# Gate and up of a feed-forward by Strassen's scheme, with its activations stored to memory between two stages

## What is computed

```python
def conv_ffn(h, conv_prev, w_gate_l, w_up_l, w_conv_l, b_conv_l, w_down_l):
    t_ = h.shape[1]
    g = jnp.einsum('btd,df->btf', h, w_gate_l)
    u = jnp.einsum('btd,df->btf', h, w_up_l)
    gp = jnp.concatenate([conv_prev.astype(g.dtype), g], axis=1)
    gc = sum(gp[:, j:j + t_] * w_conv_l[j] for j in range(CONV_W)) + b_conv_l
    a = (jax.nn.gelu(gc.astype(jnp.float32)) * u.astype(jnp.float32)).astype(h.dtype)
    return jnp.einsum('btf,fd->btd', a, w_down_l), gp[:, -(CONV_W - 1):]
```

## Time and profile before

| | us |
|---|---|
| median of 3 runs (3435.79 to 3442.96) | 3439.86 |
| the profiled execution | 3438.7 |
| its span in the profile | 3437.1 |
| PE busy in the span | 3172.0 (92%), 19515 matmuls |
| DVE busy | 2157.2 (63%) |
| ACT busy | 1555.2 (45%) |
| POOL busy | 703.7 (20%) |
| DMA | 614.89 MB, mean 179 GB/s |
| mean granted clock | 0.966 |

### The profile page before, as it was taken

One profiled execution on the slowest core, in us unless ns is written; L12 is line 12 of the kernel. 1 busy time (PEld: TensorE's weight loads), 2 busy tenths in 40 slices (PEclk: granted clock), 3 DMA queues, 4 the chain that ended last, 5 costly groups with the idle time before them and its releaser, 6 DMA issues. The chain is left out here.

```text
span 3437.1 us, 58878 instructions
## 1 busy us (share of the span) xinstructions
PE 3172.0 (92%) x19515; PEld 2946.1 (86%) x19515; DVE 2157.2 (63%) x4569; ACT 1555.2 (45%) x3302; POOL 703.7 (20%) x532
## 2 busy tenths in 40 slices
PE   6989989799989997876997999999999999999997
PEld 5989989698989994443785999999999999999997
DVE  7787776578777773333995664566366446636754
ACT  5555544588867773322543333333333343333332
POOL 4464554254510003333452000000000000000000
PEclk8999999899999998998998999999999999999999
DMA  4546556727366769997586674576467557655442
GB/s 139 155 156 184 163 156 180 201 46 157 72 147 156 180 173 293 311 318 249 163 245 190 181 231 144 162 246 211 134 206 232 162 154 234 204 159 145 122 115 81
DMA packets 670664, 614.89 MB, mean 179 GB/s; under 512 B 39849, under 2 KB 580866, under 8 KB 665282
## 3 DMA queue, kind: packets, MB, share of 16 engines
q1 hardware_dynamic: 640726, 479.02, 49.6%
q10 hardware_dynamic: 10606, 69.86, 6.0%
q0 software_dynamic: 19104, 63.06, 5.7%
HBM read 512.41 MB, written 166.40 MB: 197 GB/s over the span
## 5 line engine op out<-in xcount | busy, mean ns | idle before, releaser
L2743 DVE TENSOR_TENSOR ff_wl<-ff_wr,ff_wh 128x1024 fp32r<-128x1024 f32 (+2 forms) x380 | 403.9, 1079 | 248.3 <-ACT ff_wh L2675 248.1
L2675 ACT ACTIVATE ff_wh<-ff_wr 128x1024 fp32r<-128x1024 f32 (+2 forms) x380 | 348.8, 938 | 207.1 <-PE ff_d L2600 126.3
L2598 PE MATMUL ff_g<-ld_mem,ff_wh 128*128 128x416 f32 x880 | 311.0, 353 | 20.0 <-DVE ff_wl L2743 19.8
L2598 PE MATMUL ff_u<-ld_mem,ff_wh 128*128 128x416 f32 x880 | 310.1, 352 | 2.7 <-DVE ff_wl L2743 2.7
L2598 PE MATMUL ff_d<-ff_ah,ff_wh 128*128 128x416 f32 x880 | 312.2, 355 | 0.0
L2600 PE MATMUL ff_d<-ff_ah,ff_wl 128*128 128x416 f32 x880 | 310.0, 352 | 0.0
L2600 PE MATMUL ff_g<-ld_mem,ff_wl 128*128 128x416 f32 x880 | 309.9, 352 | 0.0
L2600 PE MATMUL ff_u<-ld_mem,ff_wl 128*128 128x416 f32 x880 | 308.8, 351 | 0.0
L2599 PE MATMUL ff_g<-ld_mem,ff_wh 128*128 128x416 f32 x880 | 308.6, 351 | 0.0
L2599 PE MATMUL ff_u<-ld_mem,ff_wh 128*128 128x416 f32 x880 | 307.7, 350 | 0.0
L2599 PE MATMUL ff_d<-ff_al,ff_wh 128*128 128x416 f32 x880 | 307.5, 349 | 0.0
(11 more groups left out here) (312 smaller groups left out, 8171.2 us busy)
## 6 DMA issues: line engine op xcount, KB each, us to landing
...
bx_kca<-in_cache_a_k SPq DMA_DIRECT2D x128, 256.0 KB, 13.5
sa_vca<-in_cache_a_v POOLq DMA_DIRECT2D x128, 256.0 KB, 8.0
...
```

Source lines behind the costliest of these rows:

```text
L2598: pe.matmul(dst[:, 0:FG], wh[:, k, c], src[0][:, c0 + c], start=first and c == 0, stop=False)
L2675: act.activation(wh[:, slot, 0:size], wr[:, slot, 0:size], ACT.Copy).then_inc(w_hi, 1)
L2743: dve.tensor_tensor(wl[:, slot, 0:size], wr[:, slot, 0:size], wh[:, slot, 0:size].bitcast(F32), ALU.subtract).then_inc(w_lo, 1)
```

## The change

The function `ffn` and its stage are taken out. In their place stand `ffn_up` (stage `fu`) and `ffn_down` (stage `fd`) inside an outer stage `fk`, which keeps what both need.

- `ffn_up` makes gate and up in the manner of the projection: three rounds of 704, 704 and 672 tokens, 22 quads in each (11 pairs of feature tiles, gate in the even quads and up in the odd ones), 84 matmuls in each quad. Unlike in the projection the sums of weights are made by DVE (`sums`, names `fu_sm`). So are the sums of tokens: of the four of the first round POOL makes three and DVE one; those of the second and third are made by DVE in quads 11, 13, 15 and 17 of the round before. The first tap is one ACT instruction with scale and bias (`first_tap`), gelu stays on ACT, taps 1 and 2 and the product of gate and up are DVE's, now 704 wide. The split of the product is gone from here. The finished activations go to a tensor `a` in memory (23.4 MB) by stores of SP (`send`). The code is unrolled. SP also issues the copies of the window caches (`roll_old`), one per quad, and later two per down tile in four of the five groups.
- `ffn_down` makes the down product as before: 5 groups of 416 tokens, 8 tiles, 22 chunks, 3 matmuls. Its input comes back from `a` in four parts per group (`load_a`), is split by ACT (`values_high`) and DVE into a ring of 5 parts (`RING`), and the parts of the weights are 6, 5, 6 and 5 chunks.
- The mix writes `h2T` as one float32 part: one copy by ACT and one by DVE for each token tile, one store. `hid` holds the first 704 tokens, unsplit; `ffn_up` makes the high and low parts of each of the seven token operands of a round itself.

```diff
-IN_PLACE = FG // P
+AHEAD = ROUNDS[0][1]
+IN_PLACE = AHEAD // P
...
+        self.hid = self.own("ahead_hid", [P, DC, AHEAD], 0)
...
-                    sp.wait_ge(low2, raised(2 * m + 2))
-                    for part, src in enumerate(staged):
-                        sp.dma_start(t["h2T"][part][:, :, m * P:m * P + r],
-                                     src[:, m % 2, :, 0:r]).then_inc(h_out[m % 2], 16)
+                    sp.wait_ge(kept_a, raised(m + 1))
+                    sp.wait_ge(kept_b, raised(m + 1))
+                    sp.dma_start(t["h2T"][:, :, m * P:m * P + r], staged[:, m % 2, :, 0:r]).then_inc(h_out[m % 2], 16)
                 if m == IN_PLACE:
-                    for part, src in enumerate(staged):
-                        sp.dma_start(hid[:, part, :, m * P:FG].bitcast(F32), src[:, m % 2, :, 0:FG - m * P]).then_inc(hid_in, 16)
+                    sp.dma_start(hid[:, :, m * P:AHEAD], staged[:, m % 2, :, 0:AHEAD - m * P]).then_inc(hid_in, 16)
...
+                act.wait_ge(turned2, raised(2 * m + 1))
+                act.activation(hidden_rows(m, 0), t2[0][:].rearrange("p (c x) -> p c x", c=4)[:, :, 0:r], ACT.Copy).then_inc(kept_a, 1)
...
+                dve.wait_ge(turned2, raised(2 * m + 2))
+                dve.tensor_copy(hidden_rows(m, 1), t2[1][:].rearrange("p (c x) -> p c x", c=4)[:, :, 0:r]).then_inc(kept_b, 1)
...
+ROLLS = [(kind, n, half) for n in range(DEC_B) for kind in range(2) for half in range(8)]
...
+def ffn_up(nc, t, ahead, keep):
...
+        ready = []
+        for i, (q, k) in enumerate(order):
+            ready.append(max([at[q - 1, k] if q >= 1 else -1, i - 7] + ready[-1:]))
+        T_ORDER = [(2, 1, 5, 3, 6, 7, 4)] + [(5, 2, 1, 3, 6, 7, 4)] * (NR - 1)
+        T_SUMS = (5, 7, 6, 4)
+        t_at = {(r, k): 7 * r + i for r in range(NR) for i, k in enumerate(T_ORDER[r])}
+        sum_at = {(r, k): 4 * r + i for r in range(NR) for i, k in enumerate(T_SUMS)}
+        S_ORDER = (5, 6, 3, 7)
...
+            def load_w(q, u):
+                if q >= TOTAL:
+                    return
+                n = 2 + u
+                if q >= n:
+                    sp.wait_ge(summed, raised(4 * (q - n) + 4))
+                    for k in ((4,) if u else (1, 2)):
+                        sp.wait_ge(w_lo, raised(at[q - n, k] + 1))
+                f = f_of(q, u) * P
+                sp.dma_start((rb if u else ra)[:, q % n], views[q % 2][:, :, f:f + P]).then_inc(w_in[u][q % n], 16)
+
+            def load_tokens(r):
+                at_, w = ROUNDS[r]
+                sp.wait_ge(t_lo, raised(7 * r))
+                for i in range(H_PARTS):
+                    c = slice(2 * i, 2 * i + 2)
+                    sp.dma_start(hraw[:, c, 0:w], t["h2T"][:, c, at_:at_ + w]).then_inc(h_in, 16)
+
+            def send(q):
+
+                for u in range(2):
+                    at_, w = ROUNDS[q // FNQ]
+                    sp.wait_ge(a_ok, raised(unit(q, u) + 1))
+                    sp.dma_start(t["a"][:, f_of(q, u), at_:at_ + w], ab[:, u, 0:w]).then_inc(keep.a_out[u], 16)
+
+            for u in range(2):
+                load_w(0, u)
+            for u in range(2):
+                load_w(1, u)
...
+            for q in range(TOTAL):
+                load_w(q + 2, 0)
+                if q % FNQ == 3 and q // FNQ + 1 < NR:
+                    load_tokens(q // FNQ + 1)
+                if q % 2 == 0 and q >= 4:
+                    send(q - 4)
+                roll_old(sp, t, keep, q)
+                load_w(q + 3, 1)
...
+            pool.memset(keep.carry[:], 0.0).then_inc(clear, 1)
+            token_sum(pool, 0, 7)
+            token_sum(pool, 0, 6)
+            token_sum(pool, 0, 4)
...
+            def tokens_high(r, k):
+                n = HALF[r]
+                if k in T_SUMS:
+                    act.wait_ge(t_sum, raised(sum_at[r, k] + 1))
+                elif r == 0:
+                    act.wait_ge(ahead.hid_in, 16)
+                else:
+                    act.wait_ge(h_in, raised(16 * H_PARTS * r))
+                if r > 0:
+                    act.wait_ge(mm, raised(at[FNQ * r - 1, k] + 1))
+                act.activation(oh[:, k - 1, :, 0:n], tokens_of(r, k), ACT.Copy).then_inc(t_hi, 1)
...
+            def first_tap(q, u):
+
+                f, w, first = f_of(q, u), prompt(q), aux_after(q, u) - (5 if last_round(q) else 2)
+                wait_unit(act, q, u)
...
+                    act.wait_ge(a_ok, raised(unit(q - 2, u) + 1))
+                n = span(q)
+                act.activation(ca[:, u, 0:n], gb[:, u, 0:n], ACT.Identity, scale=cw[:, 0, f:f + 1],
+                               bias=cw[:, TAPS, f:f + 1]).then_inc(tapped, 1)
+
+            def gelu(q, u):
+                n = span(q)
...
+            def beside(q, k):
+
+                if q % 2 == 1:
+                    if k == 5:
+                        first_tap(q - 1, 0)
+                    if k == 1:
+                        gelu(q - 1, 0)
+                if q % 2 == 0 and k == 4:
+                    first_tap(q, 1)
+                if q % 2 == 0 and q >= 2 and k == 2:
+                    gelu(q - 2, 1)
+
...
+            for j, k in enumerate(T_ORDER[0][0:5]):
+                tokens_high(0, k)
+                weights_high(j)
+            wait_mixed(act, ahead)
+            for i, (q, k) in enumerate(order):
+                read_product(q, k)
+                if i in EARLY:
+                    tokens_high(0, EARLY[i])
+                if next_round(i) is not None:
+                    tokens_high(next_round(i), k)
+                for x in range(len(order)):
+                    if ready[x] == i:
+                        weights_high(x)
+                beside(q, k)
...
+            def sums(q, k):
...
+            def beside(q, k):
+
+                if k == 3:
+                    sums(q + 2, 5)
+                for x, s_ in ((5, 6), (2, 3), (1, 7)):
+                    if k == (x if q else 5):
+                        sums(q + 1, s_)
+                if q % 2 == 1:
+                    for x, u, j in ((5, 0, 1), (2, 0, 2), (6, 1, 1)):
+                        if k == x:
+                            tap(q - 1, u, j)
+                elif q >= 2:
+                    if k == 5:
+                        tap(q - 2, 1, 2)
+                    if k == 2:
+                        gate(q - 2, 0)
+                    if k == 6:
+                        gate(q - 2, 1)
+                r, m = divmod(q, FNQ)
+                if r + 1 < NR and k == 1:
+                    for x, s_ in ((11, 5), (13, 7), (15, 6), (17, 4)):
+                        if m == x:
+                            token_sum(dve, r + 1, s_)
+
...
+D_PARTS = [6, 5, 6, 5]
+SLOTS = len(D_PARTS)
+RING = 5
...
+        PIECES = [(0, 0, 2), (0, 2, 6)] + [(p, 0, D_PARTS[p % SLOTS]) for p in range(1, PARTS)]
...
+            def load_a(p):
+                if p >= PARTS:
+                    return
+                g, j = divmod(p, SLOTS)
+                if j == 0:
+                    rounds = sum(at_ < (g + 1) * FG for at_, _ in ROUNDS)
+                    for u in range(2):
+                        sp.wait_ge(keep.a_out[u], 16 * PAIRS * rounds)
+                if p >= 2:
+                    sp.wait_ge(a_lo, raised(pieces_to[p - 2]))
+                c0 = FIRST[j]
+                sp.dma_start(ar[:, p % 2, 0:D_PARTS[j]], t["a"][:, c0:c0 + D_PARTS[j], g * FG:(g + 1) * FG]).then_inc(ar_in[p % 2], 16)
...
+                if g + 1 < NF:
+                    if d == 2:
+                        load_a(SLOTS * (g + 1))
+                        load_a(SLOTS * (g + 1) + 1)
+                    if d == 6:
+                        load_a(SLOTS * (g + 1) + 2)
+                    for i in range(2):
+                        roll_old(sp, t, keep, NR * FNQ + 2 * T + i)
...
+                weights_high(SLOTS * T + 2)
+                if d == 7:
+                    values_high(SLOTS * (g + 1) + 1)
+                if d == 0:
+                    if g == 0:
+                        values_high(2)
+                    values_high(SLOTS * g + 3)
+                if d == 3:
+                    values_high(SLOTS * (g + 1))
+                weights_high(SLOTS * T + 3)
+                if d == 7:
+                    values_high(SLOTS * (g + 1) + 2)
+                weights_high(SLOTS * T + 4)
+                weights_high(SLOTS * T + 5)
+                act.wait_ge(mm, raised(SLOTS * T + SLOTS))
...
-        ffn(nc, t, ahead)
+        with Stage(nc, "fk") as last:
+            keep = Kept(last)
+            ffn_up(nc, t, ahead, keep)
+            ffn_down(nc, t, ahead, keep)
```

960 lines of the change are left out of this document (574 added, 386 removed).

## The result

The changed kernel takes 3407.33 us (median of 5 runs, 3398.65 to 3416.45), the kernel before 3439.86 (median of 5, 3435.79 to 3450.5). The ratio is 0.9897, with a 95% interval from 0.9878 to 0.9915. So 32.5 us, 1.0%, are gained where 88.7 were forecast, and 3407 lies above the range's end of 3395. The profiled execution took 3398.65 us with a span of 3397.0, 40.1 less than the span of before. It is the fastest of the five; where runs differ is told further down.

What follows compares the result with a forecast made beforehand. TensorE was taken to bound the feed-forward, its matmul count setting the length. Terms summing to −88.7 us took the span from 3437.1 to 3348.4; with 1.6 and 1.2 us added the forecast was 3351 us, range 3325 to 3395.

Steps and rivals of the forecast that it cites:

- gate and up matmuls: Gate and up: 5544 narrower matmuls replace 5280 of 416 columns, at 0.160 and 0.1534 us each; −122.0 us (−115 to −126).
- other PE time of those halves: Old gate and up halves: slow clock after the start, transposes and short waits go with the old stage; −18.0 us.
- start (with the small transposes): Start of gate and up: 20 us lost (12 to 30) while token operands are split, +11.4; small transposes +1.5.
- two changes of round: Gate and up: seven token splits overload DVE in a round's last quad, about 5 us lost each; +10 us.
- seam and first down tile: Between gate and up and down: nothing loaded ahead, first tile ends 32 us after stage start; +27 us (14 to 40).
- the other 39 down tiles: Down stage: only four turn-backs that stood beside gate and up were priced, +1.8 us; DVE's activation splits cost nothing.
- mix, barrier, end: Mix makes two copies fewer per tile, −1 us; one more nested stage, +0.6 us.
- DVE in the steady state: Gate and up quads: DVE needs 11.8 us against PE's 13.4, so PE stays the bound; 0 us.
- rival D: Gate and up: DVE becomes the bound, its 512-wide operations at 1.035 us, +152 us, 3503 us; chance 0.04.
- rival B: Seams cost as in the projection: 17 us per change of round, 30 at start, 35 at seam; 3393 us; chance 0.17.
- down groups still at 102 to 103 us: Down stage: sign expected in the new profile, each group's time unchanged from 102.87 us before.

## Why the prediction was wrong

Against the span of before, by the prediction's own steps:

| step | forecast | measured |
|---|---|---|
| gate and up matmuls | −122.0 | −116.2 |
| other PE time of those halves | −18.0 | −14.4 (3.6 of small waits came in its place) |
| start (with the small transposes) | +12.9 | +16.9 |
| two changes of round | +10 | +9.2 |
| seam and first down tile | +27 | +26.0 |
| the other 39 down tiles | +1.8 | +41.0 |
| mix, barrier, end | −0.4 | −2.6 |
| sum | −88.7 | −40.1 |

**The matmuls.** The mechanism was right and the pitch a little off. A steady quad takes 13.53 us (0.1611 a matmul) in the first two rounds and 12.97 (0.1544) in the third: 44 × 13.53 + 22 × 12.97 = 880.7 against 874.9. I had taken 0.160 between a clean stretch and a projection quad; the measured pitch lies nearer to the quad. The 336 columns came at 0.1544 where 0.1534 was taken. The rule from the Trainium skill, page "TensorE: Matmul & The Clock Gate", section "Wait — 56ns, not 53.3ns?", that was set against this term makes the pitch 149 ns for 352 columns (an estimate by that rule); here it is 161, so the trace again disagrees.

**DVE in the steady state.** 11.8 us of 13.4 were forecast, 88%; measured 83%, a little under the 85 to 90% that the prediction named. Its conclusion was right, and with it that rival D would not come. The reason given for it, that POOL is idle, is now shown: with POOL at work, DVE instructions of 0.69 us take 3.7 and one that takes 0.95 takes 3.9. The Trainium skill, page "SBUF — State Buffer", section "Who interferes with whom", states that the two share ports under an exclusive lock. The trace agrees for these instructions, all of which read two operands in SBUF: DVE finished one per POOL instruction, 0.55 to 0.75 us after its end.

**The start and the changes of round.** The start cost 4 us more, inside its bounds: the first two quads take 20.1 us more than steady ones, and the first matmul comes 5.4 us after the first weight transfer is issued instead of 8.6. What it is made of was right (a DVE chain, long beside POOL), and taking POOL away gave back 3.7. The price of an instruction beside POOL was too low. The 2.71 us of the earlier trace rows was met beside a shorter sum; the trace of before also had splits that stood beside POOL's large sums:

```profile
207.38 3.80 DVE L584 TENSOR_TENSOR pj_wl<-pj_sm,pj_wh 128x512 fp32r<-128x512 f32 x1 [1.53 <-ACT pj_wh L485]
211.10 3.72 DVE L584 TENSOR_TENSOR pj_wl<-pj_rb,pj_wh 128x512 fp32r<-128x512 f32 x1
```

The second stands beside the sum of the earlier trace rows. The changes of round cost 4.7 and 4.5 us where 5 were said: rival B is out.

**The seam** took 38.6 us, from the end of the last product, where 39.6 was said. That is partly luck: the prediction took 6.1 MB at 201 GB/s, while from 2797.80 to 2826.00 us the transfers ran at 342 GB/s with a DMA share of 1.02 and moved 9.6 MB, the cache copies and later weights among them. And the experiment put its price in between: 6.5 of the 16.9 us before the first product went with the loads moved ahead.

**The down tiles** are where it failed: 39.2 us, four fifths of the 48.6 that were missed. The step reads "Four turn-backs that stood beside gate and up: +1.8" and, on DVE in the down groups, "Nothing", with the splits of the activations alone in view; the norm and residual of four groups have no term in it. Its own sign, down groups still at 102 to 103 us, failed too: the first eight of the 39 tiles take 103.4, but those of the second, third and fourth group 112.1 to 112.2. Before, a group's norm and residual ran beside the first four gate tiles of the next group (`beside` in `head`), a stretch in which DVE had a gate tile's time for them. Now the next group is down tiles alone, and these steps with all their instructions stand in DVE's row between the result of one tile and the weight splits of the next. I had counted DVE's busy share there (34.40 of 102.87 us, now 42.32 with the activations in it) and read it as room. It was room in the wrong place: from the turned result to the next split that TensorE needs there is the time of one part of a tile, under 3 us, of which two copies and a split already took most; 1.1 to 1.2 us were free, and 2.5 to 3.2 us of norm went in. Moving the steps by some instructions, with no work less, gave 31.9 of the 39.2 us back. Of the rest, the convolution state's copies are 2.6 (14.3 to 13.81 in five tiles) and late weights 3.6 in that profile. With all of it mended the 39 tiles take 509.1 us, within 1 us of what the prediction's +1.8 makes them.

Of the prediction's range, then: it had bounds for every cost that was named. The one that decided was set at nothing with no bound at all.

**What varies between runs** is mostly not the changed part: in the profiles the last matmul of the mix lies between 1865.7 and 1880.9 us from run to run, whatever the kernel, while gate and up of the changed kernel took 913.4 both times (912.6 to 915.2 in all five profiles in which its start is unchanged) and the down part 547.5 and 551.9 (up to 553.6 where its steps are unchanged, by the last group). The profiled run of the result is an early one (1869.8), which goes with its being 9 us under the median.
